# Spreading a projection over the stages around it: hybrid Hyena and pooling encoder layer

## The reference, cut to what matters

```python
mod = silu(c) @ w_ada + b_ada; shift, scale, gate = split(mod, 3)
u = h * (1.0 + scale) + shift
proj = u @ w_in + b_in                     # 1024 -> 3072 columns
hy_streams, hy_gate, pool_in, pool_gate = split(proj, ...)   # 1536, 512, 512, 512
k_freq = rfft(hyena_filters(...), 2 * L)   # 3-layer sine MLP of the position, times a decay
z = v                                      # v, x1, x2 = short_conv(hy_streams, 3 taps)
for o, g in enumerate((x1, x2)):
    z = g * (irfft(rfft(z, 2 * L) * k_freq[o])[:L] + bias[o] * z)
y_h = z * silu(hy_gate)
y_p = (grouped linear of (windowed mean - token)) * pool_scale * silu(pool_gate)
h = layer_norm(ALPHA * h + gate * (concat(y_h, y_p) @ w_out + b_out))
```

## Time and profile before

| | us |
|---|---|
| median of 3 runs (1505.31 to 1510.5) | 1505.89 |
| the profiled execution | 1512.34 |
| its span in the trace | 1510.6 |
| PE busy / DVE / ACT / POOL | 1226.2 / 837.5 / 461.6 / 427.1 |
| mean granted TensorE clock | 0.931 |
| DMA | 273.5 MB, mean 181 GB/s |

### The profile page before, as it was taken

One profiled execution on the slowest core, in us unless ns is written; L12 is line 12 of the kernel. 1 busy time (PEld: TensorE's weight loads), 2 busy tenths in 40 slices (PEclk: granted clock), 3 DMA queues, 4 the chain that ended last, 5 costly groups with the idle time before them and its releaser, 6 DMA issues. The chain is left out here.

```text
span 1510.6 us, 14907 instructions
## 1 busy us (share of the span) xinstructions
PE 1226.2 (81%) x5260; PEld 943.8 (62%) x5260; DVE 837.5 (55%) x784; ACT 461.6 (31%) x619; POOL 427.1 (28%) x236
## 2 busy tenths in 40 slices
PE   3788956489999999999999953784757855699996
PEld 1356734378888888888888732553545534488884
DVE  5756856563223122222144443895546966889997
ACT  3335655441212111111111132453433544411110
POOL 2111100150110122122022000673434853434445
PEclk9779989899999999999999977898897987999998
DMA  8279999951132250122012069895988959542321
GB/s 316 76 258 318 308 348 407 325 134 56 56 112 79 87 168 36 62 83 56 8 49 56 28 249 341 235 275 191 353 333 248 338 207 325 205 168 85 105 89 69
DMA packets 170488, 273.50 MB, mean 181 GB/s; under 512 B 24007, under 2 KB 70087, under 8 KB 167626
## 3 DMA queue, kind: packets, MB, share of 16 engines
q1 hardware_dynamic: 167949, 267.96, 53.0%
q0 software_dynamic: 1152, 4.19, 0.7%
q10 hardware_dynamic: 1328, 0.59, 0.2%
HBM read 180.42 MB, written 107.23 MB: 190 GB/s over the span
## 5 line engine op out<-in xcount | busy, mean ns | idle before, releaser
L136 PE MATMUL prj_pp<-u_uhi,prj_whi 128*128 128x512 f32 x768 | 300.2, 391 | 0.2 <-POOL u_ulo L800 0.2
L138 PE MATMUL prj_pp<-u_uhi,prj_wlo 128*128 128x512 f32 x768 | 299.0, 389 | 0.0
L137 PE MATMUL prj_pp<-u_ulo,prj_whi 128*128 128x512 f32 x768 | 299.0, 389 | 0.0
L136 PEld LDWEIGHTS prj_pp<-u_uhi,prj_whi 128*128 128x128 f32 x768 | 144.2, 188 | 30.6 <-issue 0.6
L138 PEld LDWEIGHTS prj_pp<-u_uhi,prj_wlo 128*128 128x128 f32 x768 | 144.2, 188 | 30.4
L137 PEld LDWEIGHTS prj_pp<-u_ulo,prj_whi 128*128 128x128 f32 x768 | 144.2, 188 | 29.5
L808 POOL CAST prj_whi<-prj_ws 128x1024 fp32r<-128x1024 f32 x22 | 23.9, 1086 | 392.5 <-DMA prj_ws<-in_w_in 230.3
L899 ACT ACTIVATE prj_row<-prj_pp,prj_bcol 128x512 f32<-128x512 f32 x64 | 43.9, 688 | 291.1 <-PE prj_pp L138 253.7
L1001 DVE TENSOR_SCALAR prj_cv<-prj_row,prj_cw,prj_cb 128x2048 f32<-128x2048 f32 x12 | 16.2, 1347 | 191.6 <-PE prj_px L844 103.9
L1284 POOL TENSOR_TENSOR sp_y<-sp_by_re,sp_by_im 128x512 f32<-128x512 f32 x32 | 68.2, 2132 | 191.1 <-DVE sp_by_im L1355 191.1
L136 PE MATMUL sp_u<-sp_ahi,spec_fwd 128*128 128x512 f32 x128 | 57.2, 447 | 62.3 <-DVE sp_alo L1335 62.3
(11 more groups left out here) (186 smaller groups left out, 2476.6 us busy)
## 6 DMA issues: line engine op xcount, KB each, us to landing
kseq<-fs_xo SPq DMA_DIRECT2D x32, 512.0 KB, 4.1
fs_a<-kseq SPq DMA_DIRECT2D x32, 512.0 KB, 8.6
kfreq<-fs_out SPq DMA_DIRECT2D x32, 512.0 KB, 9.2
sp_a<-xseq SPq DMA_DIRECT2D x32, 512.0 KB, 5.9
sp_kf<-kfreq SPq DMA_DIRECT2D x64, 256.0 KB, 5.8
bseq<-sp_out SPq DMA_DIRECT2D x32, 512.0 KB, 3.5
prj_ws<-in_w_in SPq DMA_DIRECT2D x24, 512.0 KB, 6.4
net_wa<-in_w_ada SPq DMA_DIRECT2D x8, 1024.0 KB, 12.0
```

Of the source, the lines that this page charges most:

```text
L136: nc.tensor.matmul(out, w[0], m[0], start=start, stop=False, skip_group_check=True)
L137: nc.tensor.matmul(out, w[0], m[1], start=False, stop=False, skip_group_check=True)
L138: return nc.tensor.matmul(out, w[1], m[0], start=False, stop=stop, skip_group_check=True)
```

## The change

The separate projection stage is gone. A class `Projection` holds `uhi` and `ulo`, the weights and two PSUM banks (four before) over six new stages, which replace fs2 to sp1:

- p1 (`values_and_filters`): fs2's 32 units (`unit`), forming of u in steps 0 to 7 (from a transposed x that the host lays out, no TensorE transposes), and chunks 0 to 15 (v), at the steps of `chunk_at`.
- p2 (`signal_stage1`): 16 groups, and chunks 16 to 23 (first gate pair).
- p3 (`spectrum_product`): 16 units and chunks 24 to 39 (x1), one a step, in halves.
- p4 (`between_orders`): 16 groups and chunks 40 to 47, in odd steps.
- p5 (`spectrum_product`): 16 units and chunks 48 to 63 (two gate pairs).
- p6 (`pooling`): chunks 64 to 95 and the pooling branch.

`uhi`/`ulo` take 128 KB per partition all the time, so the transform stages have fewer buffers: p1 loads 3 deep (6 before) with 2 splits (4), p3 and p5 have one tile each of `ahi`, `alo`, `y`, `yhi`, `ylo`, `out` and of both PSUM results (2 before) and loads 2 deep (4 before for `a`, 3 for `kf`); p4 is 2 deep (4) with one `xhi`/`xlo`. Weight tiles are loaded to one `ws` (2 before), from a copy that the host lays out contiguously, and all are split by POOL.

The row order of the transforms is another, so that filter generation, fs1's first step and the first steps in p2 and p4 (`fwd`) are pairs of matmuls of 64 rows each, into different banks, as `inv` of the product stages already was. fs1 has no POOL copies any more (`hs_`) and works in 16 groups times 2 orders with 3 buffers. The short convolution of turned tiles is 12 instructions on 512 elements (3 on 2048 before). All table copies of fs1 go to `front`, and `g2` is loaded to `ya` in `last_inverse` (in sp1 before). `output_norm` is as it was. The loops are written out, except in `output_norm`.

```diff
-            sp.dma_start(tabs["w1f"][0:FIRST_TABS], t["t_w1f"][0:FIRST_TABS]).then_inc(copied, 16)
...
+            for name in ("w1f", "kgen", "kfirst", "f0", "f1", "i0", "i1"):
+                sp.dma_start(tabs[name], t["t_" + name]).then_inc(copied, 16)
...
+                    for h in range(2):
+                        hs = slice(64 * h, 64 * h + 64)
+                        mm = nc.tensor.matmul(gen_ps[r][:, h, :], hfil[hs, a, g, :], wfil[hs, b, o, :],
+                                              start=part == 0, stop=part == 2 and (g > 0 or h == 1), skip_group_check=True)
...
-                    mm = mm3(nc, s1_ps[r][:, o, :], (tab[n % 4][:, 0, :], tab[n % 4][:, 1, :]),
-                             (khi[r][:, o, :], klo[r][:, o, :]), True, True)
+                for h in range(2):
+                    for part, (a, m) in enumerate(((0, khi), (0, klo), (1, khi))):
+                        for jj in range(2):
+                            js = slice(64 * jj, 64 * jj + 64)
+                            mm = nc.tensor.matmul(s1_ps[r][:, jj, :], tab[g % 3][js, h, a, :], m[r3][js, h, :],
...
+    def load_w(self, sp, n):
+        if n < len(TILES):
+            if n:
+                sp.wait_ge(self.wlo_done[(n - 1) % 2], (n - 1) // 2 + 1)
+            sp.dma_start(self.ws[:, :, :], self.t["t_win"][TILES[n], :, :, :]).then_inc(self.w_in, 16)
+
+    def split_w(self, pool, n):
+        if n < len(TILES):
+            b = n % 2
+            pool.wait_ge(self.w_in, 16 * n + 16)
+            after(pool, self.prj_done[1], 2 * n - 2)
...
+    def half_chunk(self, pe, q, half):
+        n, c, b, bank = q // 4, q % 4, q // 4 % 2, q % 2
+        if half == 0:
+            if c == 0:
+                pe.wait_ge(self.wlo_done[b], n // 2 + 1)
+            after(pe, self.bank_read[bank], q // 2)
+        cols = slice(c * CH, (c + 1) * CH)
+        for k in range(4 * half, 4 * half + 4):
+            mm = mm3(self.nc, self.pp[bank][:, :], (self.whi[b][:, k, :], self.wlo[b][:, k, :]),
+                     (self.uhi[:, k, cols], self.ulo[:, k, cols]), k == 0, k == KT - 1)
+        if half == 1:
+            mm.then_inc(self.prj_done[bank], 1)
...
+TILES = (0, 1, 2, 3, 8, 12, 4, 5, 6, 7, 9, 13, 10, 14, 11, 15, 16, 20, 17, 21, 18, 22, 19, 23)
...
+        chunk_at = {2 + 2 * q if q < 4 else 9 + 3 * (q - 4) // 2: q for q in range(16)}
+        form_at = {step: (2 * step, 2 * step + 1) for step in range(8)}
+        conv_at = {step + 2: q // 4 for step, q in chunk_at.items() if q % 4 == 3}
+        turn_at = {step + 1 + part: (i, part) for step, i in conv_at.items() for part in range(4)}
...
+            def load_x(m):
+                tc, k2 = m // 4, m % 4
+                after(sp, ulo_done[m % 4], m // 4)
+                sp.dma_start(xt[m % 4][:, :, :], xsrc[:, 2 * k2:2 * k2 + 2, tc * CH:(tc + 1) * CH]).then_inc(xt_in[m % 4], 16)
...
+            for step in range(S):
+                if 0 <= step - 1 < N:
+                    unit(step - 1)
+                q = due(chunk_at, step)
+                if q is not None:
+                    if q < 4:
+                        for m in range(4 * q, 4 * q + 4):
+                            pe.wait_ge(ulo_done[m % 4], m // 4 + 1)
+                    pj.chunk(pe, q)
+                if due(turn_at, step) is not None:
+                    tn.turn(pe, *turn_at[step])
...
+            for step in range(S):
+                if step < NU:
+                    fwd(step)
+                if step < 16:
+                    pj.half_chunk(pe, q0 + step, 0)
+                if 0 <= step - 1 < NU:
+                    inv(step - 1)
+                if step < 16:
+                    pj.half_chunk(pe, q0 + step, 1)
+                if tn and step in turn_at:
+                    i = turn_at[step]
+                    for part in range(4):
+                        if 4 * i + 6 + part // 2 == step:
+                            tn.turn(pe, i, part)
+
+        @block.scalar
...
+                nc.vector.tensor_tensor(ylo[:, :, :], y[:, :, :], f32(yhi[:, :, :]), ALU.subtract).then_inc(ylo_done, 1)
+
+            def multiply(n):
+                dve.wait_ge(u_done, n + 1)
+                dve.wait_ge(k_in[n % 2], 16 * (n // 2) + 16)
+                after(dve, ylo_done, n)
+                nc.vector.tensor_tensor(y[:, :, :], u_ps[:, :, :], kf[n % 2][:, 0:1, :].broadcast_to([P, 2, DH]),
+                                        ALU.mult).then_inc(mul_done, 1)
+                after(dve, y_done, 2 * n)
...
+            for step in range(S):
+                if step < NU:
+                    alow(step)
+                c = step - 2
+                if tn and step in conv_at:
+                    tn.conv(dve, conv_at[step])
+                if gt and 0 <= c < 16:
+                    if c % 8 == 3:
+                        gt.conv(dve, c // 8)
+                    elif c % 8 >= 4:
+                        gt.gate(dve, c // 8, c % 4)
+                if 0 <= step - 1 < NU:
+                    ylow(step - 1)
+                if step < NU:
+                    multiply(step)
...
+            for step in range(S):
+                if step < GS:
+                    inv(step)
+                c = due(chunk_at, step)
+                if c is not None:
+                    pj.half_chunk(pe, q0 + c, 0)
+                if 0 <= step - 3 < GS:
+                    fwd(step - 3)
+                if c is not None:
+                    pj.half_chunk(pe, q0 + c, 1)
...
+            for n in range(4):
+                load(n)
+            load_w(0)
+            load_w(1)
+            for k in range(4):
+                sp.dma_start(ya[:, k, :], g2[k, :, :]).then_inc(ya_in, 16)
+            for n in range(4, GS):
+                load(n)
+                if n % 2 == 1:
+                    load_w(n // 2)
+            sp.dma_start(gate_bias[:, :], rows[1, :].partition_broadcast(P)).then_inc(bias_in, 16)
+            sp.wait_ge(bias_in, 16)
...
+        with Scope(nc, "prj") as u:
+            pj = Projection(nc, t, u)
+            values_and_filters(nc, t, tabs, pj, scale1, shift, kseq, kfreq, vx)
+            signal_stage1(nc, tabs, pj, vx, xseq[0], g2)
+            spectrum_product(nc, "p3", tabs, t, pj, xseq[0], kfreq[0], bseq[0], 6, vx=vx)
+            between_orders(nc, tabs, pj, vx, bseq[0], xseq[1], g2)
+            spectrum_product(nc, "p5", tabs, t, pj, xseq[1], kfreq[1], bseq[1], 12, g2=g2)
+            pooling(nc, t, pj, yp)
 
```

More of the change, by code:

```diff
@@ L499, in _ @@
             nc.gpsimd.memset(e0[:, 0:1], 1.0).then_inc(e0_set, 1)
-            pool.wait_ge(e0_set, 2)
-            for n in range(GF):
-                after(pool, gen_done[n % 2], n // 2)
-                nc.gpsimd.tensor_copy(hs_[n % 2][:, :, :], hfil[:, :, :, n]).then_inc(hs_ready[n % 2], 1)
         @block.tensor
@@ new lines, in evac @@
+                after(dve, stored[n % 3], 16 * (n // 3))
+                nc.vector.tensor_copy(xo[n % 3][:, 1, :], ps[n % 2][:, 1, :]).then_inc(out1[n % 2], 1)
+            for step in range(S):
+                if step < GS:
+                    low(step)
+                if 0 <= step - 2 < GS:
+                    evac(step - 2)
+                c = due(chunk_at, step - 2)
+                if c is not None and c == 3:
+                    gt.conv(dve, 0)
+                if c is not None and c >= 4:
+                    gt.gate(dve, 0, c - 4)
```

1697 lines of the change are left out of this document (875 added, 822 removed).

## The result

The changed kernel takes 1440.19 us (median of 4 runs, 1438.96 to 1441.98) against 1505.83 beside it: a ratio of 0.956 (95% interval 0.954 to 0.958), 65.6 us less. The forecast of 1420 was 20 us too low, inside its range. The profiled execution took 1438.96 us with a span of 1437.2, 73.4 less than the span before. On the spans' scale the sum of stages, 1424.0, is 13.2 too low; the other 7 us of the 20 come from the two profiled executions, one 6.4 us over its median and the other 1.2 under it.

The account below looks back on a forecast made before the run. TensorE alone was taken to bound the projection, while it waited in the transform stages. Ten stage forecasts summed to 1424.0 against 1510.6, 86.6 less; from the median 1505.9 that gave 1420 us, range 1370 to 1500.

Parts of the forecast that it names:

- The bound and the offer: TensorE alone bounds the projection; in transform stages it is busy 50% to 70%, so matmuls can fill its waits.
- the change of form: p3 and p5: switching between full and half-row matmuls costs 0.1 us each, making a step 9.75 us.
- loads are issued two steps ahead: p3: loads have 19 us for a landing of 6 to 9 us.
- rival A: p3 and p5: queue neighbours lengthen a unit's chain to 20.3 us; +163, 1583 us; chance 0.07, partly 0.12.
- a chain from forward to inverse: p3: one unit's chain ends 13.3 us after the step's start, before its inverse at 15.2; TensorE stays the bound.
- The prediction's 1.9: p3: 1.9 us of slack between the end of a unit's chain and its inverse.
- The convolution: Short convolution ahead of `ylow`: up to 2 us late in four p3 steps, 4 in sum; 2 of stall in p2.
- a unit of 2.6: fs1: 32 units at 2.6 us each, 83 us of the stage's 106.
- a warning of 12 us: fs1: loads are issued only about two units ahead; if each landing shows, the stage is some 12 us longer.
- Rival B: Half-row pairs don't overlap in the new places: fs1 +48, p2 and p4 +11 each, 1490 us; chance 0.03.
- the wait for `ya`: fin: DVE waits for the `g2` load from about 10 to about 20 us; stage +13 us, to 75.
- Rival D: TensorE's clock stays low in mixed stages; at 0.92 the TensorE-bound parts cost 60 us more, 1480; chance 0.04.

Follow-up runs that it names:

- experiment 1: Changed kernel with the turned tiles' stores issued ahead of the same step's loads in p3: 1427.23 us, ratio 0.945 to the kernel before.
- experiments 2 and 3: Changed kernel with p5's chunks behind its units: 1504.89 us; on top, GpSimd's second sum cut to 16 of 512 columns in p3 and p5: span 1493.2 us.
- experiment 6: Changed kernel with fs1's loads of decay and table held five deep instead of three: 1427.68 us, ratio 0.944 to the kernel before.
- experiment 5: Changed kernel with fs1's 64-row matmuls reordered so neighbours use the same half: 1443.81 us; then all transform ones reading one half: 1563.62 us.
- experiment 7: Changed kernel with p1's chunks 4 to 15 spread to steps 9 to 29 instead of 9 to 25: 1451.33 us.

## Why the prediction held, and where it did not

*The bound and the offer.* Right: matmuls went into time in which TensorE waited. p5 shows it best, 163.0 of 177.7 us busy at clock 0.97.

*p3 and p5, the step.* 10.05 instead of 9.75. The term that was mis-sized is the change of form: 0.1 us from the one longer distance of the earlier trace rows, while a change delays two distances, 0.2 in all. That is 0.2 of a step's 0.3; the last 0.1 is that the 42 slots average 0.230 us and not 0.227. The price lies above both that the prediction weighed (0.1 and 0.16): 22 us over the 110 changes of all stages, by estimate. The Trainium skill (TensorEngine Tiling (Array Packing), Key Properties) says that changing the tiling mode drains TensorE; the trace agrees, with the 0.31 and 0.34 us above. The step's 0.3 us are 9.6 of the 20.8 us that p3 and p5 ran over.

*p3, the queue.* The step that failed is "loads are issued two steps ahead". They are; but the prediction went through SyncE's list for the loads and not for the turned tile's store, which a load holds back there. It named queues only in rival A, as a matter of every step. It struck two tiles of four, 12.4 us (experiment 1), of which the lower clock behind each wait is about 3. With the step's 4.8 that makes 193 into 210; 209.1 was measured.

*The chain and rival A.* Rival A did not happen: the inverse waited for `ylow` only behind convolutions. But the cover is thinner than the text has it. It took a chain from forward to inverse and compared it with the inverse's place; the ring through the single `y` was not looked for. The ring needs 8.36 us a step (experiments 2 and 3), so 1.7 us a step are to spare. The prediction's 1.9 is nearly that number by luck: it is the slack of another path, and that path was priced with GpSimd's two sums at 4.26 us (about 3.5 in most units here) and `ylow` at 2.04 (1.22, or 3.42 beside a weight split). Whoever makes TensorE's share smaller gains at most this a step. The interleaving is also worth more than its 23.7 us against the kernel before: against its own buffers without it, 61.2. (Rival A's sum of 20.3 is 19.8 by its own terms, and its time then 1567; that changes no argument.)

*The convolution.* Forecast at 1 us a tile; 1.6 in p3, 0.86 in p5. In p2 forecast at 2; it cost 6, and moving it gave 6.2 back, to 74.7 us against the forecast's 75.

*fs1.* The sum had both halves, a unit of 2.6 and a warning of 12 us for the distance of the loads. The unit is 2.27, and the warning was true with 14.2 us (experiment 6). The two errors nearly cancel, so that 111.2 stands close to 106 for the wrong reason. Rival B is refuted for fs1 by experiment 5.

*p1.* 12 us better: the part up to the end of chunk 3 took 67.4 instead of 69, the middle up to the end of chunk 15 95.0 instead of 99, the rest 35.4 instead of 42. The middle is the matmul streams one behind the other, as the prediction had them (93.8), without its 5 us of stalls: TensorE idled 0.6 us of the 95 (experiment 7). The largest miss is the rest, and what paces it and the first part is not settled: neither chunks at other steps (+5) nor the store's wait (-1.5) moved the stage much, and no run changed its loads.

*p4, fin, front.* p4's period was 12.1 for 12 forecast. In fin the wait for `ya` was 10.05 us, as said, but the stage is only 7.0 us longer instead of 13; what made the rest good was not looked into. The table copies in front cost nothing (-1.2 against before).

*Rival D.* Not as a steady state: p5 had 0.97. In p3 the clock fell to 0.50 twice, each time behind a wait of 4 us, and cost about 3 us. In p4 it goes with two lengths of the stage, as the last section shows.

## What to carry over

Before sharing two streams on one engine, find each stream's ring: the slowest closed path through a buffer and through the order of each queue. In p3 and p5 the shared step cost the larger of the ring and the sum of the engine's work, and the distance between the two is all that a later cut can win. When a step is too long, look at the clock as well as at the waits: here the step behind a wait paid too. Read a queue once for every kind of DMA in it, asking what stands ahead of the stores, and not only how early the loads are issued. A stage that comes out near its forecast can still hold two errors that cancel, here a unit 0.3 us too dear and loads 14 us too late.
